# Hybrid decoder layer: the far rows of the value cache loaded from GpSimd's queue instead of SyncE's

## The reference, cut to what matters

```python
def _dilated_sample(q, k_all, v_all, bias_j, dilation, n_steps, q_offset):
    T = q.shape[1]
    steps = jnp.arange(n_steps + 1)
    idx = (q_offset + jnp.arange(T))[:, None] - steps[None, :] * dilation
    ...
    vg = v_all[:, idx]
    scores = jnp.einsum('bthd,btjhd->bhtj', q, kg,
                        preferred_element_type=jnp.float32) * SCALE + bias_j.T[None, :, None, :]
    p, lse = _softmax_stats(scores, valid[None, None])
    o = jnp.einsum('bhtj,btjhd->bthd', p, vg.astype(jnp.float32))
    return o, lse.transpose(0, 2, 1)
```

## Time and profile before

| | |
|---|---|
| median of 3 runs | 1091.85 us (1089.55 to 1094.21) |
| profiled execution | 1091.73 us, its span from first to last instruction 1089.9 us |
| granted TensorE clock, mean | 0.965 |
| TensorE (PE) busy | 978.3 us, 90% |
| VectorE (DVE) busy | 275.2 us, 25% |
| ScalarE (ACT) busy | 142.4 us, 13% |
| GpSimd (POOL) busy | 27.7 us, 3% |
| DMA | 343.45 MB, mean 315 GB/s |

### The profile page before, as it was taken

One profiled execution on the slowest core, in us unless ns is written; L12 is line 12 of the kernel. 1 busy time (PEld: TensorE's weight loads), 2 busy tenths in 40 slices (PEclk: granted clock), 3 DMA queues, 4 the chain that ended last, 5 costly groups with the idle time before them and its releaser, 6 DMA issues.

```text
span 1089.9 us, 11345 instructions
## 1 busy us (share of the span) xinstructions
PE 978.3 (90%) x4851; PEld 586.3 (54%) x4851; DVE 275.2 (25%) x392; ACT 142.4 (13%) x325; POOL 27.7 (3%) x52
## 2 busy tenths in 40 slices
PE   5999999999989999999948888978999779978785
PEld 4777888887766667777734334422343224422342
DVE  2006999490233330111242101100011001200011
ACT  3011111211124440011110110001001010001000
POOL 3000000000010000000000000000000000000000
PEclk9999999999989999999978999989999889999998
DMA  9845799954739994454374999999999999999971
GB/s 323 301 160 198 266 405 386 354 191 159 269 143 354 344 350 172 155 216 182 130 287 187 381 422 421 421 422 422 421 422 423 422 422 421 422 423 422 422 325 41
DMA packets 78020, 343.45 MB, mean 315 GB/s; under 512 B 5694, under 2 KB 8952, under 8 KB 51368
## 3 DMA queue, kind: packets, MB, share of 16 engines
q1 hardware_dynamic: 59743, 296.19, 68.6%
q10 hardware_dynamic: 15408, 34.02, 8.6%
q0 software_dynamic: 2816, 12.49, 2.9%
HBM read 330.53 MB, written 11.98 MB: 314 GB/s over the span
## 4 chain that ended last, share of the span: by engine, by line
PE 69%; DMA 25%; issue 2%; DVE 1%; ACT 1%; SPq 1%; POOL 0%; ACTq 0%; POOLq 0%; DVEq 0%
PE PS L753 66%; DMA ring<-in_w_up 13%; DMA ring<-in_w_gate 5%; DMA ring<-in_w_down 2%; DMA ring<-in_w_in 2%; PE PS L783 1%; DMA x_scr<-Z 1%; DMA X<-x_scr,pidx 1%; PE PS L819 1%; PE PS L1011 1%; DVE HT L1527 0%; SPq L434 0%; DVE Z L1527 0%; ACT Z L700 0%; ACT zT L580 0%
## 5 line engine op out<-in xcount | busy, mean ns | idle before, releaser
L753 PE MATMUL PS<-HT,ring 128*128 128x288 f32 x1536 | 382.7, 408 | 1.6 <-DMA ring<-in_w_in 0.8
L753 PEld LDWEIGHTS PS<-HT,ring 128*128 128x128 f32 x1536 | 288.2, 190 | 84.9 <-issue 6.3
L753 PE MATMUL PS<-ring,Z 128*64 128x512 f32 (+2 forms) x1072 | 247.4, 604 | 33.2 <-DMA ring<-in_w_up 16.0
L753 PEld LDWEIGHTS PS<-ring,Z 128*64 128x64 f32 (+2 forms) x1072 | 87.3, 144 | 182.3 <-issue 177.7
L753 PE MATMUL PS<-ring,HT 128*64 128x512 f32 x512 | 120.1, 625 | 17.6 <-DMA ring<-in_w_up 10.3
L753 PEld LDWEIGHTS PS<-ring,HT 128*64 128x64 f32 x512 | 41.1, 143 | 90.8 <-issue 89.5
L753 PE MATMUL PS<-Z,X 128*128 128x256 f32 x160 | 51.5, 453 | 18.4 <-DMA X<-x_scr,pidx 10.8
L580 ACT ACTIVATE zT<-PS 128x288 f32<-128x288 f32 x48 | 19.7, 411 | 369.0 <-PE PS L753 337.7
L753 PEld LDWEIGHTS PS<-Z,X 128*128 128x128 f32 x160 | 40.7, 325 | 39.6 <-issue 17.0
L1527 DVE TENSOR_TENSOR HT<-PS,ln2R 128x512 f32<-128x512 f32 x24 | 16.6, 692 | 150.7 <-PE PS L753 150.7
L1587 DVE TENSOR_TENSOR Z<-Z,PS 128x512 f32<-128x512 f32 x8 | 5.5, 688 | 151.8 <-PE PS L753 151.8
(11 more groups left out here) (196 smaller groups left out, 537.2 us busy)
## 6 DMA issues: line engine op xcount, KB each, us to landing
ring<-in_w_gate SPq DMA_DIRECT2D x32, 2048.0 KB, 17.5
ring<-in_w_up SPq DMA_DIRECT2D x32, 2048.0 KB, 17.5
ring<-in_w_down SPq DMA_DIRECT2D x32, 2048.0 KB, 20.1
ring<-in_w_in ACTq DMA_DIRECT2D x12, 2048.0 KB, 16.7
ring<-in_w_o SPq DMA_DIRECT2D x8, 2048.0 KB, 12.7
ring<-in_cache_v SPq DMA_DIRECT2D x8, 1536.0 KB, 7.6
ring<-in_cache_v SPq DMA_DIRECT2D x32, 384.0 KB, 8.5
ring<-in_cache_k SPq DMA_DIRECT2D x24, 384.0 KB, 6.8
```

The costliest lines, as they stand in the source:

```text
L753: return pe.matmul(out, lhsT, rhs, start=start, stop=stop, skip_group_check=True)
```

## The change

The four far DMAs of each sequence go from SyncE's program to GpSimd's, with a semaphore pair `v_far` of their own; TensorE waits for `v_in` (now 32 for a sequence) and `v_far` (64). The conditions at which they are issued are the same. The two first sequences stand in GpSimd's program ahead of the `pool_prompt` and `pool_sample` stores, the six others behind them.

```diff
-    v_in = [sem(f"v_in{n}") for n in range(2)]
+    v_in, v_far = [sem(f"v_in{n}") for n in range(2)], [sem(f"v_far{n}") for n in range(2)]
...
             near_rows(sp, "cache_v", b, v_tile[n][:, 6, :], v_in[n])
             mid_rows(sp, "cache_v", b, v_tile[n][:, 0:3, :], v_in[n])
-            far_rows(sp, "cache_v", b, v_tile[n][:, 3:6, :], v_in[n])
...
+        for b in range(2):
+            pool.wait_ge(proj_done, 28 + 4 * b)
+            far_rows(pool, "cache_v", b, v_tile[b][:, 3:6, :], v_far[b])
         pool.wait_ge(z_moved, 3 + 24)
         pool.dma_start(o["pool_prompt"][0, 0], z[P - BUF:P, 1, 3 * AW:IN_W]).then_inc(stored, 16)
         for b in range(DEC_B):
             pool.dma_start(o["pool_sample"][0, b, BUF - DEC_T:BUF, :],
                            z[b * DEC_T:(b + 1) * DEC_T, 2, 3 * AW:IN_W]).then_inc(pstored, 16)
+
+        for b in range(2, DEC_B):
+            pool.wait_ge(o_done, b - 1)
+            far_rows(pool, "cache_v", b, v_tile[b % 2][:, 3:6, :], v_far[b % 2])
...
-            pe.wait_ge(v_in[i % 2], 96 * (i // 2 + 1))
+            pe.wait_ge(v_in[i % 2], 32 * (i // 2 + 1))
+            pe.wait_ge(v_far[i % 2], 64 * (i // 2 + 1))
```

## The result

The changed kernel takes 1094.2 us in the median, against 1091.95 us for the kernel before, 20 runs of each. The ratio is 1.0021 (1.0011 to 1.0030): some 2.3 us slower, more than the spread of the medians allows for chance, and under half of the 0.5% (5.5 us) that was set as "no change". One of the 20 runs took 1303.03 us at a mean granted clock of 0.743 and is left out of the ratio. The profiled execution took 1094.12 us with a span of 1092.3; before it was 1091.73 and 1089.9, so the spans differ by 2.4 us and that is what has to be found.

A forecast was written before the change was run, and what follows sets the result against it. TensorE was taken to set the attention loop's pace, with transfers keeping up with little in hand. 1091.73 - 0 + 0 to 0.4 gave 1091.7 to 1092.1 us, stated as 1092.0, range 1089 to 1097.

The forecast's parts named there:

- late tail: Attention loop: far rows meet the next sequence's loads and land late; mostly too little to tell, up to 1097 us; chance 0.08.
- SyncE's lost issues: SyncE's queue in the attention loop: four fewer issues per sequence, 2.56 us, with nothing waiting for them; gain 0.
- GpSimd gains 32 issues ... Cost: 0.: GpSimd in the attention loop: 0.59 us per issue, 2.4 us per sequence, hidden because GpSimd is idle; cost 0.
- TensorE's second wait: Each attention turn: one more 0.051 us instruction on TensorE's sequencer, taken as 0, or 0.4 us without cover.
- Last landing within 12.7 us of `o_done`, room some 3 us.: Attention loop: far values land by 12.7 us, TensorE needs them at 15.9 us after `o_done`; cost 0.
- the good one: Bound on the last landing: all transfers together keep 370 GB/s, so the batch ends 11.6 to 12.7 us after `o_done`.
- the bad one, 12.6 us: Bound on the last landing: GpSimd's far rows get 106 GB/s beside SyncE's loads, then 228 GB/s alone.
- the gather's quarter: GpSimd queue's share beside SyncE's loads, taken from a gather at 106 GB/s while 421 GB/s move.
- VectorE's copy out of PSUM: During the issue of sequence 2: a 0.41 us copy might delay GpSimd's far rows by 0.4 us; cost 0.
- narrow queue: Attention loop: GpSimd transfers can't exceed 106 GB/s even alone, so landings slip each turn; 1115 to 1129 us, chance 0.08.
- the 153: Mark for the GpSimd queue in GB/s: below it, 1.57 MB of far rows need more than a 10.28 us turn.

The follow-up runs named there:

- The first kernel with tiny copies: The kernel before plus 32 copies of 64 bytes on GpSimd behind its `pool_sample` stores, no value load moved: 1109.24 us, ratio 1.0162.

## Why the prediction came out as it did

The forecast was 1092.0 us in a range of 1089 to 1097, "the same". The measured 1094.2 and +0.21% lie in both, but the loss is clear of chance and the sum had nothing for it. Most of the reasons stood and one step was wrong. That the forecast held all the same owes something to luck: the missed price was under half of the 5.5 us that would have mattered, and the range was wide for other reasons, the spread of the runs and a late tail.

- **SyncE's lost issues: gain 0.** Held. Only lines 328 and 318 are issued for a sequence, and nothing behind them came sooner to any effect.
- **"GpSimd gains 32 issues ... Cost: 0."** This step failed. The issue was sized well: 0.566 to 0.589 us each and 2.27 to 2.30 for a sequence, where 0.59 and 2.4 stood, and it is hidden as said; the store of `pool_prompt` was issued at 315.21 (315.52 before), not pushed back. What was missed is a second price of the same instruction, paid 700 us later: 32 x 0.082 = 2.6 us in GpSimd's DRAIN, on the path that ends the program, with no other work to cover it. The row was there before the change (3337 ns at 1086.4), but in none of the views that were read: it counts as no busy time and stands in neither the chain nor the groups of the page. "Engine idle" was taken as "free to issue". With this price the sum is 1091.73 + 2.61 = 1094.3, against 1094.12 profiled and 1094.2 in the median.
- **TensorE's second wait: 0 to 0.4 us.** Held; two semaphores alone are at 0.9993.
- **Last landing within 12.7 us of `o_done`, room some 3 us.** Nearly held: 13.5 us for sequence 4, room 2.3, and 12.5 to 13.2 us with some 3 us of room for the other five. The cost of 0 stands. Of its two bounds the good one was read from sequence 4 alone and the bad one, 12.6 us, summed for a batch by itself, so neither holds for all: before, sequence 7 already took 381.9 + 9.8 - 377.67 = 14.0 us, and now the far rows of sequence 3 land at 349.1, 2.6 us into the turn in which sequence 4 is issued. The share was mis-sized. With the gather's quarter near and middle rows would have been in after 7.9 us of transfer and the far rows alone behind them. In fact both end within 0.2 us of each other, so the far rows had about their part of the bytes, 1.57 of 3.67 MB, 0.43. The Trainium skill ("DMA: Bandwidth & Descriptors", Queues, rings and completion order) says that each DMA engine takes turns between the queues that have work, packet by packet. Even turns would be a half; this trace lies nearer to that than to the quarter, and the measured 0.43 decides. The share that a gather had beside weight loads did not carry over to these loads.
- **VectorE's copy out of PSUM.** The 0.41 us were inside the room either way; GpSimd's four issues of this turn took 2.30 us, 0.03 more than those of the next turns, so the copy did not hold them up for its length.
- **Rival "narrow queue", 1115 to 1129.** Refuted: the far rows' 1.57 MB are in 13.2 us after the first issue (346.8 to 360.0), 119 GB/s. That is under the 153 that the prediction set as the mark, but beside 2.10 MB of the other queue, which the mark left out. What decides is that no turn got longer, that the last landing stays at 12.5 to 13.5 us after `o_done` instead of growing by 4.5 us a turn, and that GB/s in the turns stay at 318 to 366. (In its sum the landing of sequence 2 at 342.5 has 1.0 us over 326.7 + 14.8 that nothing accounts for.) Its chance was rightly small. The first kernel with tiny copies shows what a starved loop looks like.
- **Rival "late tail", to 1097.** Did not happen: no cache transfer is in the chain. It would have been easy to take the +2.3 us for it, since it offered a loss of about this size in the stretch that was edited. Turns equal to 0.01 us and the loss that went with the DRAIN tell that it isn't.

## What to carry to other kernels

An idle engine is not a free DMA queue. On GpSimd, count the DMAs since its last DRAIN and add 0.08 us for each to the end of the program, where that engine finishes last; issue the same bytes in fewer DMAs there (8 instead of 32 took back 1.96 of 2.61 us). Where it idles earlier, an added DRAIN takes the cost out of the end: this one line made the kernel before 0.25% faster (0.11 to 0.40%), about as much as the change lost. And when a small loss appears, look at the last 10 us of the span and at instructions that count as no busy time before blaming the stage that was edited.

## What the runs showed of the hardware that was not expected

- GpSimd's DRAIN takes 0.134 us behind one DMA and 5.95 us behind 72, 0.082 us for each, whatever their size, though all have landed before it starts (the last scatter at 1085.0, the DRAIN at 1086.1). What it does in this time no run shows. The DRAINs of the other engines, SyncE's with most of the kernel's transfers behind it among them, take 0.06 to 0.08 us.
- 32 copies of 64 bytes on GpSimd's queue, issued among value loads, brought the rate of all transfers to 29 GB/s for 10 us while the DMA engines counted as 0.60 busy, and one load landed 23.71 us after its issue had ended. Issued where nothing else was being moved, the same copies kept the engines busy for only 0.02 to 0.04, and held loads up again as soon as these began (12 GB/s at a share of 0.53, from 313 to 316). Why was not tried.
- With two queues in the loop the rate as a whole stayed about as it was, and the last landing stayed at 12.5 to 13.5 us after `o_done` (11.7 to 14.0 before). The middle rows of sequence 4 landed 12.9 us after issue in place of 7.4, together with the far rows.
